# A streaming-encoder block with 16,384 experts: low parts of the expert tiles later in a head, four more early products, another tail

## What is computed

```python
def _peer(h, w_query, sub_keys, expert_down, expert_up):
    q = (xt @ w_query).reshape(T, PEER_HEADS, 2, D_HALF)
    s = jnp.einsum('thpd,hpnd->thpn', q, sub_keys).astype(jnp.float32)
    top_s, top_i = lax.top_k(s, PEER_TOPK)
    cand = (top_s[:, :, 0, :, None] + top_s[:, :, 1, None, :]).reshape(T, PEER_HEADS, PEER_TOPK * PEER_TOPK)
    best_s, best_c = lax.top_k(cand, PEER_TOPK)
    ...
    ids = (i1 * N_KEYS + i2).reshape(T, PEER_HEADS * PEER_TOPK)
    gates = jax.nn.softmax(best_s, axis=-1)
    ...
        a = jnp.einsum('tkd,td->tk', expert_down[idb], xb)
        act = jax.nn.gelu(a.astype(jnp.float32), approximate=False).astype(xb.dtype) * gb
        return jnp.einsum('tk,tkd->td', act, expert_up[idb])
```

## Time and profile before

| what | us |
|---|---|
| median of 3 runs (1597.95 to 1600.35) | 1598.69 |
| the profiled execution, its own time | 1596.62 |
| its span in the trace | 1594.8 |
| PE busy | 1488.6 (93%) |
| DVE busy | 1194.6 (75%) |
| ACT busy | 628.5 (39%) |
| POOL busy | 680.8 (43%) |
| mean granted clock of PE, share of full | 0.978 |
| moved by DMA | 390.55 MB, mean 245 GB/s |

### The profile page before, as it was taken

One profiled execution on the slowest core, in us unless ns is written; L12 is line 12 of the kernel. 1 busy time (PEld: TensorE's weight loads), 2 busy tenths in 40 slices (PEclk: granted clock), 3 DMA queues, 4 the chain that ended last, 5 costly groups with the idle time before them and its releaser, 6 DMA issues.

```text
span 1594.8 us, 26301 instructions
## 1 busy us (share of the span) xinstructions
PE 1488.6 (93%) x7670; PEld 1277.6 (80%) x7670; DVE 1194.6 (75%) x2435; ACT 628.5 (39%) x1026; POOL 680.8 (43%) x715
## 2 busy tenths in 40 slices
PE   3999997998769999969999999999999999999994
PEld 3575545987659999958888888888888888888883
DVE  6546437799986788748787777778777787777777
ACT  1114324544346777623333333333333333333322
POOL 0000011566445666626444444455445444445461
PEclk9999998999979999989999999999999999999998
DMA  9962301332124799899999999998999999998984
GB/s 331 361 224 106 106 26 39 102 118 99 55 75 161 203 237 238 229 331 364 309 317 317 314 321 312 311 315 313 318 315 318 311 320 312 314 314 307 312 270 151
DMA packets 248575, 390.55 MB, mean 245 GB/s; under 512 B 119576, under 2 KB 165728, under 8 KB 248416
## 3 DMA queue, kind: packets, MB, share of 16 engines
q1 hardware_dynamic: 112704, 230.50, 42.4%
q0 software_dynamic: 36864, 134.23, 24.1%
q10 hardware_dynamic: 98976, 25.43, 7.0%
HBM read 353.80 MB, written 36.31 MB: 245 GB/s over the span
## 4 chain that ended last, share of the span: by engine, by line
PE 68%; DVE 9%; issue 4%; DMA 1%; ACT 1%; POOL 1%; DVEq 0%; ACTq 0%; POOLq 0%; SPq 0%
PE bank L1668 11%; PE bank L1667 10%; PE bank L1666 10%; PE bank L1609 10%; PE bank L1611 10%; PE bank L1610 10%; PE bank L1644 5%; DVE topi L1156 2%; DVE dlo L1165 1%; DVE top L1153 1%; DVE score L1160 1%; DMA gates_dram<-stage 1%; DVE pick L1176 1%; DVE bests L1153 1%; DMA rows_d<-in_peer_down,idx_d 0%
## 5 line engine op out<-in xcount | busy, mean ns | idle before, releaser
L1609 PE MATMUL bank<-h2hi,dhi 128*128 128x384 f32 x1024 | 348.1, 340 | 32.3 <-DVE dlo L1165 32.3
L1611 PE MATMUL bank<-h2hi,dlo 128*128 128x384 f32 x1024 | 345.1, 337 | 0.0
L1610 PE MATMUL bank<-h2lo,dhi 128*128 128x384 f32 x1024 | 344.6, 337 | 0.0
L1666 PE MATMUL bank<-uhi,ahi 128*128 128x512 f32 x768 | 302.9, 394 | 25.3 <-DVE ulo L1323 25.3
L1668 PE MATMUL bank<-uhi,alo 128*128 128x512 f32 x768 | 304.1, 396 | 0.0
L1667 PE MATMUL bank<-ulo,ahi 128*128 128x512 f32 x768 | 303.4, 395 | 0.0
L1609 PEld LDWEIGHTS bank<-h2hi,dhi 128*128 128x128 f32 x1024 | 194.3, 190 | 38.4 <-DVE dlo L1165 25.0
L610 POOL DMA_INDIRECT rows_u<-in_peer_up,idx_u x128 | 168.7, 1318 | 104.2 <-POOL idx_u L608 97.4
L1165 DVE TENSOR_TENSOR dlo<-down,dhi 128x1024 fp32r<-128x1024 f32 x128 | 179.0, 1399 | 45.4 <-ACT dhi L772 42.0
L1610 PEld LDWEIGHTS bank<-h2lo,dhi 128*128 128x128 f32 x1024 | 194.3, 190 | 4.2
L1611 PEld LDWEIGHTS bank<-h2hi,dlo 128*128 128x128 f32 x1024 | 194.0, 189 | 0.0
(11 more groups left out here) (203 smaller groups left out, 2196.6 us busy)
## 6 DMA issues: line engine op xcount, KB each, us to landing
down<-in_down_t SPq DMA_DIRECT2D x128, 512.0 KB
up<-in_peer_up SPq DMA_DIRECT2D x128, 512.0 KB, 5.0
ada<-in_w_ada SPq DMA_DIRECT2D x12, 2048.0 KB, 16.3
gate<-gates_dram SPq DMA_DIRECT2D x128, 192.0 KB
gates_dram<-stage ACTq DMA_DIRECT2D x5, 4096.0 KB, 25.3
gel_dram<-gel SPq DMA_DIRECT2D x46, 192.0 KB, 2.1
gele<-gel_dram SPq DMA_DIRECT2D x44, 192.0 KB
wq<-in_peer_query SPq DMA_DIRECT2D x16, 512.0 KB, 4.0
```

What stands on the lines that cost most here:

```text
L1609: pe.matmul(bank[7 * s][:, 0:TD], dhi[s][:, k, :], h2hi[:, k, 0:TD], start=k == 0, stop=False)
L1610: pe.matmul(bank[7 * s][:, 0:TD], dhi[s][:, k, :], h2lo[:, k, 0:TD], start=False, stop=False)
L1611: last = pe.matmul(bank[7 * s][:, 0:TD], dlo[s][:, k, :], h2hi[:, k, 0:TD], start=False, stop=k == KT - 1)
L1666: pe.matmul(got[:], ahi[j][:, tokens], uhi[j][:, half], start=first, stop=False)
```

## The change

It does these things. Line numbers in its listing differ by 10 to 45.

1. **dlo moves.** `halves` makes no dlo any more; `sums(h)` makes dlo 2h+2 and 2h+3 between the search of the candidates and `select`. Dlo 0 and 1 are made before the heads. The last head makes dlo 16 and 17 between its two searches and 18 and 19 in its `sums`, 20 and 21 follow ahead of the softmax's sum.
2. **BETWEEN goes from 6 to 10.** Early tiles go from 46 to 50; down products 16 to 21 stand before the transposes of the picks (before: 16 and 17) and four behind them, as before. ROUNDS falls to 39, early tiles with open up products after the rounds (`LATE`) rise from 4 to 10.
3. **Last gates.** ACT's last turn of each 64 tokens issues the store of the gates before the gelu and dhi of its early tile. The turns are written out instead of looped.
4. **Picks.** Dots of the first three picks come before the rounds, so that additions and dots run one group of three earlier in every round. In the tail they stand one by one between the ten late tiles.
5. **The last two up products** are made by token block: all four half blocks of block 0 for both tiles, then block 1, then block 2.

```diff
-PER_HEAD, BETWEEN, TURNS = 2, 6, TD // (2 * TB)
+PER_HEAD, BETWEEN, TURNS, AFTER = 2, 10, TD // (2 * TB), 0
...
+LATE = EARLY - ROUNDS - 1
+GROUPS_LEFT = -(-PICKS // SLOTS) - (ROUNDS + 1)
+
+
+def late(i):
+    return ROUNDS + 1 + i, i % SLOTS, i // SLOTS + (ROUNDS + 1 if i % SLOTS == 0 else ROUNDS)
...
-            sp.wait_ge(dve_ulo[0], ROUNDS + 2)
-            load_up(ROUNDS + 4, 0)
-            load_gate(ROUNDS + 4, 0)
-            load_gel(ROUNDS + 4, 0)
+            for i in range(SLOTS, LATE):
+                n, j, use = late(i)
+                sp.wait_ge(dve_act[j], use)
+                load_gate(n, j)
+                sp.wait_ge(dve_ulo[j], use)
+                load_up(n, j)
+                load_gel(n, j)
...
-            for s in range(2):
-                early(IN_HEADS - 2 + s, s)
+            for s in range(4):
+                early(IN_HEADS - 2 + s, s % 2)
             act.wait_ge(dve_bsub, 1)
...
+                    for u in range(2):
+                        gates_out(w, i, u)
+                        if t < TURNS - 1:
+                            hot_rows(2 * t + u + 2, u)
+                    if i == TURNS_C - 1:
+                        store_turns(w)
+                    early(FIRST_G + t, t % 2)
...
-            def halves(h):
-                for s in range(2):
-                    down_lo(2 * h + s, s)
+            def halves(h, last=False):
+                for s in range(2):
+                    if last and s == 1:
+                        for n in range(IN_HEADS, IN_HEADS + 2):
+                            down_lo(n, n % 2)
...
                 top16(lambda b: cand[:, b], lambda b: bests[:, b, :], lambda b: besti[:, b, :])
+                for s in range(2):
+                    down_lo((IN_HEADS if final else 2 * h) + 2 + s, s)
                 if not first:
                     select(h - 1)
...
             for s in range(2):
-                down_lo(IN_HEADS + s, s)
+                down_lo(IN_HEADS + 4 + s, s)
             ve.wait_ge(act_gexp, 1)
...
+            late_activations(0)
+            for i in range(LATE):
+                if i + 1 < LATE:
+                    late_activations(i + 1)
+                q, k = ROUNDS + 1 + i // SLOTS, i % SLOTS
+                if q <= ROUNDS + GROUPS_LEFT:
+                    gathered(q, k, last=SLOTS * q + k >= PICKS)
+                n, j, use = late(i)
+                parts_lo(j, use)
...
+            def multiply_up_last(slots):
+                for j, c in slots:
+                    up_ready(j, c)
+                for b in range(GB):
+                    for j, c in slots:
+                        for q in (2 * b, 2 * b + 1):
+                            done = up_part(j, q, last=j == slots[-1][0])
+                            if j == slots[-1][0]:
+                                done.then_inc(pe_y, 1)
```

More of the change, by code:

```diff
@@ L869, in store_chunk, with store_turns @@
                               stage[w % 2][:, keys_1, :]).then_inc(signal, 16)
[L871 to L884, removed]
+            def store_turns(w):
                 act.wait_ge(act_g, (w + 1) * (CHUNK_T // 4))
@@ L920, in round_ @@
                     down_hi(a + 2, 0)
[L921 to L922 removed]
+                gelu_dots(r + 1, SLOTS * r + SLOTS)
                 parts_hi(0, r + 1)
@@ L928, in round_ @@
                     parts_hi(j, r, first=first)
+            for n in range(AFTER_G, EARLY - 2):
+                early(n, n % 2)
             parts_hi(0, 0, first=True)
+            for n in range(max(AFTER_G, EARLY - 2), EARLY):
+                early(n, n % 2)
             act.wait_ge(stored[0], 16 * (CHUNKS // 2))
@@ L1215, in sums @@
                 ve.tensor_tensor(b, place[:], start[:], ALU.subtract).then_inc(dve_pair, 1)
+            for s in range(2):
+                down_lo(s, s)
             halves(0)
             sums(0, first=True)
-            with ve.Fori(1, PH) as h:
+            with ve.Fori(1, PH - 1) as h:
                 ch.enter(h - 1, HEAD_STEPS)
@@ L1222, in _ @@
                 sums(h)
-                ch.leave(PH - 1)
+                ch.leave(PH - 2)
+            halves(PH - 1, last=True)
+            sums(PH - 1, final=True)
             first = best[:, :, :, 0:1].broadcast_to([P, NB, PH, TOPK])
@@ L1260, in _ @@
                 hot_rows(u, u)
-            for n in range(IN_HEADS + 4, FIRST_G + 1):
+            for n in range(IN_HEADS + 8, FIRST_G + 1):
                 down_lo(n, n % 2)
@@ L1622, in _ @@
                 head(h)
-            for n in range(IN_HEADS - 2, IN_HEADS + 2):
+            for n in range(IN_HEADS - 2, IN_HEADS + 6):
                 multiply_down(n, n % 2)
@@ L1630, in _ @@
                 last.then_inc(pe_pick, 1)
-            for n in range(IN_HEADS + 2, FIRST_G):
+            for n in range(IN_HEADS + 6, FIRST_G):
                 multiply_down(n, n % 2)
@@ L1690, in _ @@
                 multiply_up(j, ROUNDS - 1)
-            multiply_up(0, ROUNDS + 1)
-            for j in range(1, SLOTS):
-                multiply_up(j, ROUNDS)
-            multiply_up(0, ROUNDS + 2, last=True)
+            for i in range(LATE - 2):
+                n, j, use = late(i)
+                multiply_up(j, use)
+            multiply_up_last([late(i)[1:] for i in (LATE - 2, LATE - 1)])
 _INS = ["x", "c", "w_ada", "b_ada", "g_pre_mix", "g_post_mix", "g_pre_ffn", "g_post_ffn", "w_in", "attn_sinks",
```

130 lines of the change are left out of this document (77 added, 53 removed).

## The result

The change made the kernel **slower**: 1605.3 us (median of five runs) against 1598.7, ratio 1.0049 (95% interval 1.0037 to 1.0060). I had forecast 1588.8, range 1580 to 1598, and faster with 0.83. The profiled run has a span of 1603.3 where my sum gave 1584.9: 18.4 to explain.

What follows compares the result with a forecast made beforehand. TensorE, busy 93% of the span, was taken as the bound, with gains only in its gaps. Terms +15 - 16.7 - 3 - 25.0 + 19.8 = -9.9 on the earlier median 1598.7 gave 1588.8, range 1580 to 1598.

Steps and rivals of the forecast that it cites:

- 1, low parts in the second half: Heads: moving dlo gains nothing per head (24.2 against 24.4); late first ring and long last head delay gate products, +15.
- One such wait is hidden by the ring: Heads: one small sum's wait for POOL's instruction costs nothing; three would give 24.8 a head; 24.2 taken.
- the ring: Heads: dependency loop from sums over POOL, PE, ACT and DVE back to the end of sums, 23.5 per head.
- some more where a gap lowers PE's clock: Heads: an addition to the 23.5 per head; first matmul after a gap takes 0.69 instead of 0.33.
- My third rival: Heads: all three small sums blocked by POOL, 24.8 a head, gates' start +18.5, 1592.3 in all; chance 0.25.
- The promised signs: Heads: dlo of 1.2, DVE still about 24, PE waiting 2 to 3.5 a head for the weights' low part.
- 2, four more early products: Rounds: four down products (46 to 50 early) move into PE's gaps around the picks, two rounds fewer, -16.7.
- 3, the gates go out earlier: Gates to rounds: last gates stored before the last early tile's gelu, -3, bounds -4 and +3.
- gates, PE start: Gates to rounds: after stores issue up to 3.9 earlier, gates and PE's start follow.
- 4, six up products: Rounds: late tiles go from 4 to 10, so six up products leave the rounds, -25.0.
- 5, the tail: After the last down product: 11.2 + 45.6 of DVE + 6 of stalls + 18.7, against 61.7 today, +19.8.
- bound by transfers: Tail: 15.5 MB move at 245 GB/s instead of 345, stalls 21 instead of 6, 1603.8 in all; chance 0.07.

Runs made afterwards that it cites:

- selections first: On the changed kernel, the selection of the head before put ahead of the three small sums; 1591.5 us, ratio 0.9956 to the kernel before.
- stores behind: On the changed kernel, all four stores of the last gates put back behind the last early tile's gelu; 1607.9 us, ratio 1.0069 to the kernel before.

## Why the prediction was wrong, by its steps

**1, low parts in the second half: +15 forecast, +21.2 measured.** The end of sums(0) came at 296.3 (forecast 295.9). The period was 24.8 on average, not 24.2: +3.7 over six heads. The sentence that failed is "One such wait is hidden by the ring". Two of the three sums were held, for 3.3 in all, and DVE's own head became 24.36 (three of the six heads), more than the ring's 23.5: that is 1.0 of the 3.7. In the other three heads dhi came late, 4.8 in all (less 2.3 of holding that the sixth head was spared); those are the heads with PE's clock at 0.50 for 3.4. Without the 1.7 that this costs they would take 23.5 to 23.6, my ring, so the ring's length was right. I had named this ("some more where a gap lowers PE's clock") and given it no number.

My third rival stood at 24.8 with a chance of 0.25, and the average is 24.8 as well, but by luck. Its mechanism is nearly the one seen: the sums are over when POOL's work is (13.5 after the head before), whether two or three are held. Its price counted twice the 0.6 that the sums take anyway: 21.0 + 3.9 - 0.6 is 24.3. The last head took 30.5 (forecast 29.4), the way to the transposes 21.5 (21.3). And I had rounded a sum of 16 to 15. The promised signs, dlo of 1.2, DVE at 24 and waits for the weights' low part of 2.2 to 3.1, all came; they did not tell the two cases apart.

**2, four more early products: right.** Two rounds went, and with the six late tiles of term 4 the stretch of the rounds shrank by 39.9 (forecast 41.7); 1.2 of the difference is the first up product, 7.14 instead of 5.98: its matmuls start 0.43 apart until 729.9, at a granted clock of 0.50, and 0.23 from there. The longer wait alone does not explain this: in selections first PE waits 18.9 as well and runs at that clock for 3.1 instead of 5.9.

**3, the gates go out earlier: -3 forecast, +4.1 measured.** The largest error, and outside my bounds (-4 to +3). The step that failed is "gates, PE start": I followed the stores' completion only. The stores went out 3.7 earlier, counted from the gate products' start, and the gates still landed 0.6 later than with the stores behind. On ACT's list the gelu of the last early tile went from the front of the stores to behind them, and SP's list has the store of that gelu ahead of the gate loads. The gathers that the early dots release I had bounded at 7, and then gave them almost nothing in the term. With two stores behind the gelu and the dots behind the first up tile, G to U is 204.3, below the 205.5 of the kernel before; each edit alone leaves it at 207.6 and 208.7.

**4, six up products: right**, in the count above; it is not measured apart from term 2.

**5, the tail: +19.8 forecast, +23.1 measured.** DVE's work (45.4), its start (11.1 after the last down product) and the end behind y (18.7) are as worked out (the 45.6 is itself a slip: its terms add up to 45.9). Stalls were 9.5 instead of 6, inside the bounds, but of another kind: not rows, as I asked readers to look for, but gel tiles queued behind up tiles. The rival "bound by transfers" gave 1603.8, near the result, by a mechanism that is not there: its 21 of stalls did not come, and the tile loads' order took most of them away.

The sum was also blind to a choice: the step from 48 to 50 early products takes 20.4 from the stretch of the rounds and gives back 8.6 at the gates, 1.5 from G to U and 17.3 in the tail, 6.8 too much by the profiles and 5.7 by the medians. The parts were all in my terms; I never summed them per step.

## What to carry to other kernels

When an instruction moves on one engine, list every other engine's queue whose next entry waits for what now stands behind it; a row of DMA issues can be such an instruction (14 us of ACT here), and its length is to be read from the queue's rows, not from the bytes. Place two-input VectorE instructions where GpSimd rests and fill GpSimd's busy time with one-input ones; moving one kind of victim out of the busy time only moves another in. Price the last pass of a loop by the engine that is left alone in it, not by the engine that bounds the loop.

## What the runs showed of the hardware

The issue of the last chunk's four gate stores (4 MB together, pieces of 256 bytes) held ACT's queue for 13.0 in all in the kernel before, 14.2 in the change and 22.5 with the stores behind, where gathers ran beside them; SP was held for 12.7 by two stores of 3 MB together. It is not the bytes that hold the engine. The five chunks before the last go out in one store of 4 MB each, with the same pieces, and the queue has such a store off its hands in 0.38, 24 before it lands:

```profile
667.48 0.38 ACTq L881 DMA_DIRECT2D gates_dram<-stage  x1
```

Of the four in a row the first takes 0.38 as well, and those behind it 3.6 to 13.5 each in these three kernels. I read this as: a large store holds the engine when it is issued behind one that is still going out. Whether fewer and larger stores at the end would free ACT sooner than they delay the gates was not tried.

One-input selections (1.21 each alone, rows 4) took 2.35 for two while POOL's two-input instruction ran through them (353.13 to 355.55). The Trainium skill, "SBUF — State Buffer", section "Who interferes with whom", says that `tensor_reduce` never contends on this chip. The trace agrees.
